# RWKV-7 / MLA / ConvGLU step: folded 64x64 inverse, alternating sample products, passes written out

## The reference

```
xn = rmsnorm(x);  P = xn @ w_in                 # columns: RWKV | MLA | branch gates
A = rwkv7_mix(P_rwkv)                           # 16 heads of 64, state S (64 x 64) per head
B = mla_attention(P_mla)                        # 8 heads
h = x + (sigmoid(Ga) * A + sigmoid(Gb) * B) @ w_out
y = h + conv_glu(rmsnorm(h));  out = rmsnorm(y)

# inside rwkv7_mix, per head and token
sa = S @ kk_t
S  = S * w_t + outer(v_t, k_t) - outer(sa, kk_t * a_t)
y_t = S @ r_t
```

## Time and profile before

| | before |
|---|---|
| median of 3 runs | 2604.16 us |
| the profiled execution | 2600.29 us, its span 2598.6 us |
| matrix engine busy | 2524.0 us (97%), 15308 matmul records |
| weight loads busy | 2324.6 us (89%) |
| vector engine busy | 1174.2 us (45%), scalar engine 870.2 us (33%) |
| chain that ended last | matrix engine 93%, vector engine 3% |
| mean granted clock of the matrix engine | 0.989 of full |

### The profile page before, as it was taken

One profiled execution on the slowest core, in us unless ns is written; L12 is line 12 of the kernel. 1 busy time (PEld: TensorE's weight loads), 2 busy tenths in 40 slices (PEclk: granted clock), 3 DMA queues, 4 the chain that ended last, 5 costly groups with the idle time before them and its releaser, 6 DMA issues.

```text
span 2598.6 us, 40216 instructions
## 1 busy us (share of the span) xinstructions
PE 2524.0 (97%) x15308; PEld 2324.6 (89%) x15308; DVE 1174.2 (45%) x1823; ACT 870.2 (33%) x1279; POOL 108.7 (4%) x182
## 2 busy tenths in 40 slices
PE   6999999999999999999999899999999999999997
PEld 6888888888888999999987799999878999999886
DVE  4566556666543333234433544444333444444233
ACT  4433233333233332234423433333222333333232
POOL 3000000000001010000000000000000000000010
PEclk9999999999999999999999999999999999999999
DMA  5321122221254343334443344444333444444433
GB/s 172 91 70 53 56 69 68 61 69 49 54 132 118 98 120 100 90 106 122 128 162 126 93 128 128 123 129 123 119 126 126 128 123 129 125 125 133 139 124 130
DMA packets 414493, 283.46 MB, mean 109 GB/s; under 512 B 31728, under 2 KB 392690, under 8 KB 413408
## 3 DMA queue, kind: packets, MB, share of 16 engines
q1 hardware_dynamic: 405600, 259.16, 33.7%
q0 software_dynamic: 8832, 23.43, 3.3%
HBM read 275.62 MB, written 6.92 MB: 109 GB/s over the span
## 4 chain that ended last, share of the span: by engine, by line
PE 93%; DVE 3%; issue 1%; ACT 1%; DMA 1%; POOL 0%; DVEq 0%; SPq 0%; POOLq 0%; ACTq 0%
PE banks L1402 19%; PE banks L846 17%; PE banks L848 17%; PE banks L847 17%; PE banks L315 3%; PE banks L421 2%; PE banks L432 2%; PE banks L857 2%; PE banks L858 2%; PE banks L859 2%; PE banks L1268 1%; PE banks L388 1%; PE banks L1265 1%; PE banks L509 1%; PE banks L1363 1%
## 5 line engine op out<-in xcount | busy, mean ns | idle before, releaser
L836 DVE TENSOR_TENSOR w_lo<-w_raw,w_hi 128x1024 fp32r<-128x1024 f32 x482 | 590.2, 1225 | 971.2 <-ACT w_hi L831 969.9
L846 PE MATMUL banks<-x_hi,w_hi 128*128 128x384 f32 x2640 | 914.5, 346 | 7.4 <-DVE w_lo L836 7.4
L848 PE MATMUL banks<-x_hi,w_lo 128*128 128x384 f32 x2640 | 885.7, 335 | 0.0
L847 PE MATMUL banks<-x_lo,w_hi 128*128 128x384 f32 x2640 | 885.3, 335 | 0.0
L831 ACT ACTIVATE w_hi<-w_raw 128x1024 fp32r<-128x1024 f32 x482 | 511.3, 1061 | 1038.8 <-PE banks L848 594.3
L846 PEld LDWEIGHTS banks<-x_hi,w_hi 128*128 128x128 f32 x2640 | 497.8, 189 | 22.6 <-DVE w_lo L836 9.3
L847 PEld LDWEIGHTS banks<-x_lo,w_hi 128*128 128x128 f32 x2640 | 497.7, 189 | 4.8
L848 PEld LDWEIGHTS banks<-x_hi,w_lo 128*128 128x128 f32 x2640 | 497.1, 188 | 0.0
L1402 PE MATMUL banks<-w_hi,act_hi 128*128 128x512 f32 x528 | 164.9, 394 | 4.7 <-DVE h_rows L1958 2.4
L1402 PE MATMUL banks<-w_lo,act_hi 128*128 128x512 f32 x528 | 164.8, 393 | 0.0
L1402 PE MATMUL banks<-w_hi,act_lo 128*128 128x512 f32 x528 | 163.7, 391 | 0.0
(11 more groups left out here) (391 smaller groups left out, 2547.6 us busy)
## 6 DMA issues: line engine op xcount, KB each, us to landing
w_raw<-in_w_ffn_in SPq DMA_DIRECT2D x176, 512.0 KB, 3.9
w_raw<-in_w_in SPq DMA_DIRECT2D x144, 512.0 KB, 3.8
w_raw<-in_w_ffn_down SPq DMA_DIRECT2D x88, 512.0 KB, 3.6
w_raw<-in_w_out SPq DMA_DIRECT2D x32, 512.0 KB, 3.4
w_raw<-in_w_o_a SPq DMA_DIRECT2D x16, 512.0 KB, 4.4
w_raw<-in_w_o_b SPq DMA_DIRECT2D x16, 512.0 KB, 3.9
w_raw<-in_w_in SPq DMA_DIRECT2D x20, 256.0 KB, 3.7
w_ukv_head<-in_w_ukv POOLq DMA_DIRECT2D x8, 512.0 KB, 4.1
```

What stands on the lines that cost most here:

```text
L836: nc.vector.tensor_tensor(lo[:, s], raw[:, s], hi[:, s].bitcast(F32), ALU.subtract).then_inc(lo_done, 1)
L846: nc.tensor.matmul(out, hi[:, s, k, :], xh[:, kt, :], start=kt == 0, stop=False)
L847: nc.tensor.matmul(out, hi[:, s, k, :], xl[:, kt, :], start=False, stop=False)
L848: last = nc.tensor.matmul(out, lo[:, s, k, :], xh[:, kt, :], start=False, stop=kt == 15)
```

## The change

- **Folded blocks.** `t_y`, `t_x`, `t_g` and `n_t` become 128 x 64 per unit: partitions 0 to 63 hold the first 64 x 64 block of the diagonal (j = 0), partitions 64 to 127 the second (j = 1), and the masks are folded alike. Each product of the inverse is then two matmuls of 64 x 64 in place of one of 128 x 128, each in its own quarter of the array: rows and columns 0 to 63 for j = 0, 64 to 127 for j = 1 (in the first product, the row half goes by the head and the column half by j). The transposes become float32 matmuls with the identity (`turned`), so two records each.
- **The full matrix** that the later steps need is put together in a new buffer `t_full`: the vector engine's last subtraction is two instructions of 64 partitions, and the scalar engine has two small copies for the samples. `t_full` is cleared once at the start.
- **Sample products** take the two heads in turn (b outside, i inside).
- **Passes written out.** The matrix engine's program for the 8 passes is straight code; waits are on constants. The vector and scalar engines keep their loops.
- **Waits ahead of the last matmul of a piece.** Inside the inverse a wait stands before the sixth matmul of the piece ahead (`at_last`) instead of before the group behind it.

```diff
@@ -198,8 +203,8 @@
         kp_ = region("kappa", [P, NT])
-        n_t, t_x, t_y, t_g, m_t, c_k, c_b = [
-            region(n, [P, 6, P]) for n in ("n_t", "t_x", "t_y", "t_g", "m_t", "c_k", "c_b")]
+        n_t, t_x, t_y, t_g = [region(n, [P, 6, 64]) for n in ("n_t", "t_x", "t_y", "t_g")]
+        t_f, m_t, c_k, c_b = [region(n, [P, 6, P]) for n in ("t_full", "m_t", "c_k", "c_b")]
...
@@ -339,7 +344,10 @@
         LEVELS = ("lv2", "lv4", "lv8", "lv16", "lv32")
-        units = lambda lv: [(i, t) for t in range(3 if lv < 3 else 2) for i in range(2)]
+        units = [(i, t) for t in range(3) for i in range(2)]
+        blocks = lambda lv: [(i, t, j) for t in range(3 if lv < 3 else 2) for i in range(2) for j in range(2)]
+        small = lambda b, i, t, j: ps[64 * j:64 * j + 64, b + i, 64 * t:64 * t + 64]
+        made_small = lambda b, n, r=slice(0, P): ps[r, b:b + 2, 0:64 * n].rearrange("p h (t c) -> p h t c", t=n)
...
@@ -371,6 +379,9 @@
             last.then_inc(E("s0_ps"), 1)
+        def turned(out, in_, j):
+            return nc.tensor.matmul(out, in_, ident[heads(j), heads(j)], start=True, stop=True)
...
@@ -383,63 +394,64 @@
             pe.wait_ge(E("gates_done"), f + 1)
-            for i in range(2):
-                for b in range(NB):
+            for b in range(NB):
+                for i in range(2):
...
-            for i, t in units(0):
-                last = mm_(head_tile(6, i, t), be[heads(i), tile_tok(t)], al[heads(i), i, tile_tok(t)],
-                           start=True, stop=True)
+            for i, t, j in blocks(0):
+                own = slice(128 * t + 64 * j, 128 * t + 64 * j + 64)
+                last = mm_(small(6, i, t, j), be[heads(i), own], al[heads(i), i, own], start=True, stop=True)
...
             pe.wait_ge(E("bonus_done"), f + 1)
-            for i, t in units(0):
+            for i, t in units:
...
             last.then_inc(E("mt_ps"), 1)
-            pieces(1)
-            pe.wait_ge(E("t_first_done"), f + 1)
-            for i, t in units(0):
-                last = transpose(head_tile(2, i, t), t_y[:, 3 * i + t, :])
+            pieces(1, lambda: pe.wait_ge(E("t_first_done"), f + 1))
+            for i, t, j in blocks(0):
+                last = turned(small(2, i, t, j), t_y[heads(j), 3 * i + t, :], j)
             last.then_inc(E("form_ps"), 1)
-            pieces(1)
-            pe.wait_ge(E("nt_done"), f + 1)
+            def matrix_ready():
+                pe.wait_ge(E("nt_done"), f + 1)
+                pe.wait_ge(E("form_done"), f * 5 + 1)
+            pieces(1, matrix_ready)
             for lv in range(5):
-                if lv == 0:
-                    pe.wait_ge(E("form_done"), f * 5 + 1)
+                def level_ready():
+                    pe.wait_ge(E("g_done"), f * 5 + (lv + 1))
+                    if lv == 0:
+                        pe.wait_ge(E("mt_done"), f + 1)
+                    else:
+                        pe.wait_ge(E("form_done"), f * 5 + (lv + 1))
+                if lv:
+                    for i, t, j in blocks(lv - 1):
+                        last = turned(small(2, i, t, j), t_x[heads(j), 3 * i + t, :], j)
+                    last.then_inc(E("form_ps"), 1)
+                for i, t, j in blocks(lv):
+                    u, h = 3 * i + t, heads(j)
+                    last = mm_(small(g_bank(lv), i, t, j), n_t[h, u, :], t_x[h, u, :], start=True, stop=True)
+                last.then_inc(E("g_ps"), 1)
+                pieces(1, level_ready)
+                if lv < 4:
+                    for i, t, j in blocks(lv):
+                        u, h = 3 * i + t, heads(j)
+                        last = mm_(small(10 - g_bank(lv), i, t, j), t_y[h, u, :], t_g[h, u, :], start=True, stop=True)
                 else:
-                    pe.wait_ge(E("t_done"), f * 5 + lv)
-                    for i, t in units(lv - 1):
-                        last = transpose(head_tile(2, i, t), t_x[:, 3 * i + t, :])
-                    last.then_inc(E("form_ps"), 1)
-                for i, t in units(lv):
-                    u = 3 * i + t
-                    last = mm_(head_tile(g_bank(lv), i, t), n_t[:, u, :], t_x[:, u, :], start=True, stop=True)
-                last.then_inc(E("g_ps"), 1)
-                pieces(1)
-                pe.wait_ge(E("g_done"), f * 5 + (lv + 1))
-                if lv == 0:
-                    pe.wait_ge(E("mt_done"), f + 1)
-                else:
-                    pe.wait_ge(E("form_done"), f * 5 + (lv + 1))
-                if lv < 4:
-                    for i, t in units(lv):
-                        u = 3 * i + t
-                        last = mm_(head_tile(10 - g_bank(lv), i, t), t_y[:, u, :], t_g[:, u, :], start=True, stop=True)
-                else:
-                    for i, t in units(lv):
-                        u = 3 * i + t
-                        last = mm_(head_tile(2, i, t), t_g[:, u, :], t_y[:, u, :], start=True, stop=True)
+                    for i, t, j in blocks(lv):
+                        u, h = 3 * i + t, heads(j)
+                        last = mm_(small(2, i, t, j), t_g[h, u, :], t_y[h, u, :], start=True, stop=True)
...
                 if lv < 4:
-                    pieces(1)
+                    pieces(1, lambda: pe.wait_ge(E("t_done"), f * 5 + (lv + 1)))
...
             for b, src in ((4, kp_), (6, be)):
-                for i, t in units(0):
+                for i, t in units:
...
@@ -473,13 +485,13 @@
                 for i in range(2):
-                    last = mm_(ps[r0:r0 + 64, 3, heads(i)], t_y[:, 3 * i + t, cs], rr[:, 0, heads(i)],
+                    last = mm_(ps[r0:r0 + 64, 3, heads(i)], t_f[:, 3 * i + t, cs], rr[:, 0, heads(i)],
...
                     for i in range(2):
-                        last = mm_(ps[:, 7, heads(i)], t_y[:, 3 * i + 2, :], rr[:, 1, heads(i)], start=True, stop=True)
+                        last = mm_(ps[:, 7, heads(i)], t_f[:, 3 * i + 2, :], rr[:, 1, heads(i)], start=True, stop=True)
...
@@ -587,16 +600,18 @@
             act.wait_ge(E("form_ps"), f * 5 + 1)
-            fn(t_x[:, :, :].rearrange("p (h t) c -> p h (t c)", h=2), ps[:, 2:4, 0:NT], ACT.Copy).then_inc(E("form_done"), 1)
+            fn(by_head(t_x, 3), made_small(2, 3), ACT.Copy).then_inc(E("form_done"), 1)
...
             for lv in range(1, 5):
-                n = NT if lv < 4 else 2 * P
+                n = 3 if lv < 3 else 2
                 act.wait_ge(E("form_ps"), f * 5 + (lv + 1))
-                fn(t_y[:, :, :].rearrange("p (h t) c -> p h (t c)", h=2)[:, :, 0:n], ps[:, 2:4, 0:n], ACT.Copy)\
-                    .then_inc(E("form_done"), 1)
+                if lv == 3:
+                    for j in range(2):
+                        fn(t_f[heads(j), 2:6:3, heads(j)], ps[heads(j), 2:4, 128:192], ACT.Copy)
+                fn(by_head(t_y, n), made_small(2, n), ACT.Copy).then_inc(E("form_done"), 1)
...
@@ -720,23 +735,26 @@
             dve.wait_ge(E("nt_ps"), f + 1)
-            link(tt(by_head(t_y, 3), made(6, 3), each(cm["nl1"], 3), M))
-            tt(by_head(t_y, 3), by_head(t_y, 3), each(ident, 3), A).then_inc(E("t_first_done"), 1)
-            masked(n_t, 6, M_S).then_inc(E("nt_done"), 1)
+            link(tt(by_head(t_y, 3), made_small(6, 3), each(fold["nl1"], 3), M))
+            tt(by_head(t_y, 3), by_head(t_y, 3), each(fold["ident"], 3), A).then_inc(E("t_first_done"), 1)
+            tt(by_head(n_t, 3), made_small(6, 3), both(M_F), M).then_inc(E("nt_done"), 1)
...
             for lv in range(5):
-                n = len(units(lv)) // 2
+                n = 3 if lv < 3 else 2
                 dve.wait_ge(E("g_ps"), f * 5 + (lv + 1))
-                tt(by_head(t_g, n), made(g_bank(lv), n), each(cm[LEVELS[lv]], n), M).then_inc(E("g_done"), 1)
+                tt(by_head(t_g, n), made_small(g_bank(lv), n), each(fold[LEVELS[lv]], n), M).then_inc(E("g_done"), 1)
...
                 if lv < 4:
-                    tt(by_head(t_x, n), by_head(t_x, n), made(10 - g_bank(lv), n), S).then_inc(E("t_done"), 1)
+                    tt(by_head(t_x, n), by_head(t_x, n), made_small(10 - g_bank(lv), n), S).then_inc(E("t_done"), 1)
                 else:
-                    tt(by_head(t_y, n), by_head(t_y, n), made(2, n), S).then_inc(E("t_done"), 1)
+                    for j in range(2):
+                        h = heads(j)
+                        last = tt(by_head(t_f, 2)[h, :, :, h], by_head(t_y, 2)[h], made_small(2, 2, h), S)
+                    last.then_inc(E("t_done"), 1)
...
@@ -845,6 +863,8 @@
                 nc.tensor.matmul(out, hi[:, s, k, :], xl[:, kt, :], start=False, stop=False)
+                if at_last and k == ks[-1]:
+                    at_last()
...
@@ -1172,33 +1192,25 @@
-            with pe.Fori(0, FT - 1) as f:
-                done = 0
-                def pieces(n):
+            done = 0
+            def next_pieces(f):
+                def pieces(n, at_last=None):
...
                         q, s, part = piece // 8, piece // 4 % 2, piece % 4
```

(21 more changed lines are left out.)

30 lines of the change are left out of this document (18 added, 12 removed).

## The result

The changed kernel takes 2559.16 us (median of 4 runs, 2552.51 to 2561.33) against 2604.09 in the runs beside it: a ratio of 0.9825, 95% interval 0.9805 to 0.9844. The forecast was 2562 us, within 2555 to 2576. A second series gave 2556.05 us (5 runs) and the same ratio, 0.9809 to 0.9842.

What follows compares the result with a forecast made beforehand. The prediction took the passes as bound by the matrix engine's own stream: -44.2 us in eight passes, +0.65 for the memset and +1.0 for fetching make -42.5, from 2604.16 to 2562 us, range 2555 to 2576.

Steps and rivals of the forecast that it cites:

- Quarters side by side: Groups of the inverse: records in quarters differing in rows and columns run at once, 0.058 us per two-record step.
- Bodies: Groups of the inverse, from their start to the next piece: folded blocks change them by -3.67 us per pass.
- Ways in: Gap from a piece's last matmul to the next group: 0.27 us everywhere, -0.20 us per pass in sum.
- Late answers: Rival: vector or scalar answers in the ten groups 0.1 us late at the moved wait, 8 us lost, 2570 us; chance 0.08.
- First product: Pass's first product, 24 records in four quarters: between -0.18 and +0.17 us per pass, taken as 0.
- Samples: Sample products with heads in turn: -0.69 us for the state products, -0.96 (-1.18 to -0.75) for the outputs, per pass.
- Per pass: Sum over one RWKV pass: -5.52 us, so -44.2 us in eight passes.
- Written-out passes: Matrix engine's straight code: removing the loop costed at nothing, fetching seven more copies at +1.0 us, or 0 without it.
- The memset: Start of the kernel: the added clearing of 768 elements delays the awaited w_lo, +0.65 us once.
- Serial quarters: Rival: the array takes the diagonal's two quarters one after the other, +9.3 us per pass in the inverse, 2642 us; chance 0.05.
- alternation without gain: Rival: taking the sample products' heads in turn gains nothing, 13.2 us fall away, 2575 us; chance 0.03.
- time given back by the pieces: Rival: small groups save, but pieces wait for w_lo; half the gain lost would be 2583 us; chance 0.04.

Runs made afterwards that it cites:

- run 3: Changed kernel with each group of the inverse ordered one quarter after the other, first product unchanged: passes of 79.03 us against 73.10.
- run 9: Changed kernel with the second head's blocks on the other two quarters in levels 2 to 4: 2535.87 us, ratio 0.9748 to the kernel before.
- run 2: Changed kernel with the inverse's waits in front of each group again, behind the sixth matmul of the piece: passes of 73.08 us against 73.10.
- run 6: Kernel before with only the matrix engine's passes written out: passes of 78.87 us, 2604.14 us in one run.
- run 4: Changed kernel with the matrix engine's first seven passes as a hardware loop again: 2614.24 us against 2602.98 for the kernel before.
- run 1: Changed kernel with the sample products of one head behind those of the other again: passes of 74.53 us against 73.10.
- run 7: Changed kernel with the memset of t_full moved from the start to about 73 us: first pass starts at 106.37 us against 107.15.
- run 5: Kernel before, loop kept, first 16 sample products done seven times over: first pass 94.51 us, later ones 101.8 to 104.7.

## Why the prediction was right, step by step

- **Quarters side by side.** Right, though no row had shown it, and the base of it all (runs 3 and 9). Bodies, measured from start to next start: form +0.21 (+0.12 forecast: the six transposes took 0.63, not 0.72), level 1 and D of levels 1 to 3 -2.06 (-2.08), transposes and G of levels 2 and 3 -0.85 (-0.86), level 4 -0.41 (-0.43), level 5 -0.54 (-0.42, since its D was taken like level 4's, but it cost 0.98 before). Sum -3.65 against -3.67.
- **Ways in.** -0.22 against -0.20. The reason given was half right: the shorter vector operation does it, the moved wait does nothing (run 2). Late answers as a rival: none here, one of 0.07 with four quarters.
- **A small miss**: the first to the last start of a piece takes 0.98 behind a tiled group and took 0.96, +0.2 per pass, which I had left out.
- **First product.** -0.16, at the lower end of -0.18 to +0.17: four quarters run side by side. I took the middle; an order of both rows and columns in turn should have been taken at the end where all overlap. The 25 ns between two starts that the prediction quotes do not hold for records in different quarters: the 24 take 0.51 with the way out, the starts of one step lie 0.006 to 0.007 us apart in the trace, and the earlier trace rows had two starts 0.01 apart already.
- **Samples.** -0.72 (-0.69) and -1.15 (-0.96; the lower bound was -1.18): the eight records of 128 columns overlap almost wholly, 0.49 (366.93 to 367.42) where 0.44 to 0.87 was forecast.
- **Per pass** -5.71 against -5.52, so -45.7 against -44.2. The first product and the sample outputs, both priced at the middle of their bounds, account for that and more; the piece's 0.2 goes against it.
- **Written-out passes: wrongly weighed.** I costed the loop that goes at nothing and its replacement at up to +1.0. For the kernel before this is so (run 6: +0.6, which the -5.71 per pass already holds). For the folded passes the loop would have cost about 8 us in each of six passes (run 4) and turned the gain into a loss. The sum came out because the change has both parts; the price of a part was not the same beside the others.
- **The memset.** 0.8 for the wait (0.65 forecast, read from a large memset to a small one behind it). I had not reckoned with the clock: 1.4 more where it falls.
- **The sum, and luck in it.** Passes and start together make -45.7 + 2.2 = -43.5; -42.5 was forecast. That close it is in part by luck: with its +1.0 for fetching the forecast gave the passes 2.5 us too little, and the start cost 1.5 us more than forecast. The 44.9 us between the medians also hold what the clock does behind the passes, up to 4.3 us in one execution, so that they lie near the forecast says little on the mechanism.
- **Rivals.** Serial quarters would have shown groups of about 1.5; 1.36, nearly that, was measured only in run 3, where the order makes them serial; alternation without gain is refuted by run 1; time given back by the pieces did not occur.

## What to carry to other kernels

Small float32 matmuls like these (64 x 64 with 64 columns, or 128 rows and 64 output columns with 16) are priced by steps, not by records: up to four records in four different quarters of the array, or two in two column halves, pass in one step of 0.058 us, if they stand next to each other in the program. Cutting products into quarters without interleaving them gains nothing. When a change makes a loop's body longer, look for instruction packets in every pass and for waits on "issue" at the loop's head before blaming the arithmetic.

## What the runs showed that was not expected

- The matrix engine stood still 3.7 to 4.9 us at the head of a loop whose body had grown from 628 to 827 or 820 matmul records, in every pass of the loop from the second on, and then ran at the lower clock (6.56 us in the fourth pass of run 4).
- The same MLA instructions took 531.2, 532.9 or 535.6 us, in kernels of either kind, with the matrix engine busy all the time; the difference is in how often the granted clock fell to 0.50.
- Behind one and the same wait of 1.87 us the clock stayed full (three profiles) or fell (run 7), and likewise behind 2.68 us (full in run 4, a fall in seven profiles).
- Products of 16 columns, 224 records in a row (run 5), ran at the lower clock while the engine never paused.
